# Attention heads in pairs: even and odd products issued in turn, wider blocks, shared banks

## The reference

```
moba:            p = softmax(mask(q k^T));                       o = p v
stick-breaking:  z = q k^T / 8;  log_beta = log_sigmoid(z)
                 later = reverse cumsum over keys of log_sigmoid(-z), the key itself left out
                 w = mask(exp(log_beta + later));                o = w v
forgetting:      z = q k^T / 8 + F[q] - F[k];  p = softmax(mask(z));  o = p v
out:             heads side by side @ w_o
```

## Time and profile before

| | us |
|---|---|
| median of 3 runs | 895.12 |
| lowest, highest | 892.17, 897.29 |
| profiled execution, own time | 894.86 |
| its span | 892.6 |
| PE busy in it | 862.9 |
| DVE busy in it | 646.9 |
| ACT busy in it | 491.5 |

### The profile page before, as it was taken

One profiled execution on the slowest core, in us unless ns is written; L12 is line 12 of the kernel. 1 busy time (PEld: TensorE's weight loads), 2 busy tenths in 40 slices (PEclk: granted clock), 3 DMA queues, 4 the chain that ended last, 5 costly groups with the idle time before them and its releaser, 6 DMA issues. The chain is left out here.

```text
span 892.6 us, 17122 instructions
## 1 busy us (share of the span) xinstructions
PE 862.9 (97%) x6968; PEld 823.1 (92%) x6968; DVE 646.9 (72%) x1332; ACT 491.5 (55%) x1015; POOL 21.2 (2%) x53
## 2 busy tenths in 40 slices
PE   6999998999999999999999997999999999999998
PEld 5788887999999999999999997878878999999998
DVE  5666666988998886999887868653634798666551
ACT  6744535777666666655545555543534676555441
POOL 1000000000000000000000007000000000000000
PEclk9999999999999999999999999977999999999999
DMA  9765365665665986699987875331304549755550
GB/s 303 245 189 184 103 190 188 215 204 197 212 208 170 314 290 211 202 316 356 308 304 258 279 232 142 116 119 48 117 25 143 189 143 329 237 189 178 189 177 24
DMA packets 151070, 179.46 MB, mean 201 GB/s; under 512 B 5712, under 2 KB 141136, under 8 KB 150992
## 3 DMA queue, kind: packets, MB, share of 16 engines
q1 hardware_dynamic: 149536, 177.65, 60.6%
q10 hardware_dynamic: 432, 0.68, 0.2%
q0 software_dynamic: 1024, 0.03, 0.1%
HBM read 177.27 MB, written 1.05 MB: 200 GB/s over the span
## 5 line engine op out<-in xcount | busy, mean ns | idle before, releaser
L894 DVE TENSOR_TENSOR wlo<-raw,whi 128x512 fp32r<-128x512 f32 x528 | 342.4, 683 | 60.5 <-ACT whi L659 59.7
L1257 PE MATMUL bank<-A,whi 128*128 128x256 f32 x1280 | 369.3, 289 | 14.1 <-DVE wlo L894 8.6
L659 ACT ACTIVATE whi<-raw 128x512 fp32r<-128x512 f32 x528 | 308.6, 621 | 110.8 <-PE bank L1259 101.9
L1258 PE MATMUL bank<-A,whi 128*128 128x256 f32 x1280 | 360.6, 282 | 0.0
L1259 PE MATMUL bank<-A,wlo 128*128 128x256 f32 x1280 | 360.4, 282 | 0.0
L1257 PEld LDWEIGHTS bank<-A,whi 128*128 128x128 f32 x1280 | 246.7, 193 | 18.5 <-issue 9.3
L1258 PEld LDWEIGHTS bank<-A,whi 128*128 128x128 f32 x1280 | 245.0, 191 | 1.0 <-issue 1.0
L1259 PEld LDWEIGHTS bank<-A,wlo 128*128 128x128 f32 x1280 | 244.8, 191 | 0.0
L1257 PE MATMUL bank<-Hhi,whi 128*128 128x256 f32 x528 | 147.0, 278 | 0.0
L1259 PE MATMUL bank<-Hhi,wlo 128*128 128x256 f32 x528 | 146.7, 278 | 0.0
L1258 PE MATMUL bank<-Hlo,whi 128*128 128x256 f32 x528 | 146.7, 278 | 0.0
(11 more groups left out here) (157 smaller groups left out, 920.8 us busy)
## 6 DMA issues: line engine op xcount, KB each, us to landing
mring<-in_w_mod SPq DMA_DIRECT2D x72, 512.0 KB, 6.0
raw<-in_ffn_w_up SPq DMA_DIRECT2D x22, 1024.0 KB, 5.1
raw<-in_w_gate SPq DMA_DIRECT2D x22, 1024.0 KB, 5.7
raw<-in_w_up SPq DMA_DIRECT2D x22, 1024.0 KB, 5.5
raw<-in_w_down SPq DMA_DIRECT2D x16, 1024.0 KB, 5.8
raw<-in_w_in SPq DMA_DIRECT2D x12, 1024.0 KB, 5.5
raw<-in_moba_w_qkv SPq DMA_DIRECT2D x11, 1024.0 KB, 6.3
raw<-in_ffn_w_down SPq DMA_DIRECT2D x8, 1024.0 KB, 7.2
```

The costliest lines, as they stand in the source:

```text
L659: act.activation(whi[:, i % SPL, k0:k1, 0:width], raw[:, i % RAW, k0:k1, 0:width], ACT.Copy).then_inc(s_whi, 1)
L894: dve.tensor_tensor(lo, raw[:, i % RAW, k0:k1, 0:width], hi.bitcast(F32), ALU.subtract).then_inc(s_wlo, 1)
L1257: pe.matmul(o, hi, xh, start=kg == 0, stop=False)
L1258: pe.matmul(o, hi, xl, start=False, stop=False)
```

## The change

Heads enter in pairs, every second call of `attend` at the earliest, and a pair's scores are issued ahead of the older pairs' steps. `scores` and `values` of both heads of a pair are issued product by product in turn, and a pair's transposes are spread over ages 2 and 3, `values` come at age 5. The scores' three blocks are laid in another order, so that one mask product of 256 columns (the same 128 twice) serves both diagonal blocks, and the stick-breaking scores and the `later` sums take one wide product in place of two or three narrow ones; values take two products a head in place of three. Scores have four banks (4, 5, 1, 3). For that the projections of the four phases around attention put both halves of a group into one bank, 0 or 2 (`halved`, `at`), apart from the first three groups of the phase `qkv3`. A padding is longer so that the buffers keep their places.

```diff
-LAST_AGE = 4
+LAST_AGE = 5
-S_BANKS = (4, 5)
+S_BANKS = (4, 5, 1, 3)
+HALVES = ("qkv1", "o1", "qkv3", "o3")
...
             if age == 0:
                 st.put("scores", n)
-            elif age == 1 and kind != "sb":
-                st.put("scale", n)
-            elif age == 2:
-                st.put("later" if kind == "sb" else "turn", n)
-                self.w_of[n] = len(self.w_of) + 1
+            elif age == 1:
+                st.put("stsum" if kind == "sb" else "scale", n)
+            elif age in (2, 3):
+                m = n + age - 2
+                st.put("later" if kind == "sb" else "turn", m)
+                self.w_of[m] = len(self.w_of) + 1
...
             old = list(flight)
-            if waiting and waiting[0][0] == "sb":
+            if waiting and (not flight or flight[-1][1] > 1):
                 enter()
-                for head in old:
-                    advance(*head)
-                st.put("stsum", flight[-1][0])
-                return
-            for head in old:
-                advance(*head)
-            if waiting:
-                enter()
+            for pair in old:
+                advance(*pair)
...
-        def pair_of(g):
-            return (0, 1) if g % 2 == 0 else (2, 3)
+        def halved(g):
+            return groups[g][0] in HALVES and g not in unnormed
+
+        def at(g, i, c0=0, c1=S):
+            if halved(g):
+                return banks[2 * (g % 2)][:, i * S + c0:i * S + c1]
+            return banks[2 * (g % 2) + i][:, c0:c1]
...
+            def first_passes(n):
+                first_pass(n)
+                first_pass(n + 1)
...
+            def peaks(n):
+                if heads[n][0] != "sb":
+                    peak(n)
+                    peak(n + 1)
...
+            def scales(n):
+                scale(n)
+                scale(n + 1)
...
+                for m in (n - 4, n - 3):
+                    if m in soft:
+                        need.wait_ge(s_exp, soft[m])
+                    elif m in stick:
+                        need.wait_ge(s_lb, stick[m])
...
+                if kind == "sb":
+                    for o0, o1, k0, q0 in ((P, 3 * P, 0, 0), (0, P, P, P)):
+                        for b, q, k in pair:
+                            pe.matmul(b[:, o0:o1], k[:, k0:k0 + P], q[:, q0:S], start=q0 == 0, stop=False)
+                    for b, q, k in pair:
+                        ins = pe.matmul(b[:, 0:S], identb[:, :], negs[:, :].unsqueeze(1).broadcast_to([P, 2, P]), start=False, stop=True)
+                        ins.then_inc(s_scores, 1)
+                    return
+                for o0, o1, q0 in ((0, S, P), (S, 3 * P, 0)):
+                    for b, q, k in pair:
+                        pe.matmul(b[:, o0:o1], q[:, q0:q0 + P], k[:, 0:o1 - o0], start=o0 == 0, stop=False)
+                if kind == "fox":
+                    i = (h - 8) // 2
+                    for o0, o1, q0 in ((0, S, P), (S, 3 * P, 0)):
+                        for e in range(2):
+                            r = slice(64 * e, 64 * e + 4)
+                            pe.matmul(pair[e][0][:, o0:o1], FA[r, i, q0:q0 + P], FB[r, i, 0:o1 - o0], start=False, stop=False)
+                for b, q, k in pair:
+                    ins = pe.matmul(b[:, P:3 * P], identb[:, :], negb[:, :].unsqueeze(1).broadcast_to([P, 2, P]), start=False, stop=True)
+                    ins.then_inc(s_scores, 1)
...
-                pe.matmul(b[:, 0:P], upn[:, :], spl[:, 0:P], start=True, stop=True)
-                pe.matmul(b[:, P:S], upn[:, :], spl[:, P:S], start=True, stop=False)
-                pe.matmul(b[:, P:S], negf[:, :], spl[:, S:S + P], start=False, stop=True)
-                pe.matmul(b[:, S:S + P], upn[:, :], spl[:, S:S + P], start=True, stop=True).then_inc(s_tpe, 1)
+                pe.matmul(b[:, 0:3 * P], upn[:, :], spl, start=True, stop=False)
+                pe.matmul(b[:, S:3 * P], negf[:, :], spl[:, 0:P], start=False, stop=True).then_inc(s_tpe, 1)
...
+                for t, o0, w0, w1 in ((0, 0, P, 3 * P), (1, P, 0, P)):
+                    for e in range(2):
+                        o, w = banks[O_BANK][64 * e:64 * e + 64, o0:S], W8[:, 2 * ((n + e) % 4) + 1, w0:w1]
+                        ins = pe.matmul(o, Vn[:, t, (h + e) * 64:(h + e) * 64 + 64], w, start=t == 0, stop=t == 1)
+                ins.then_inc(s_val, 1)
```

More of the change, by code:

```diff
@@ L227, in attend @@
         def attend():
-            for head in flight:
-                head[1] += 1
+            for pair in flight:
+                pair[1] += 1
             if flight and flight[0][1] == LAST_AGE:
@@ L599, in _ @@
             put(negb[:, :], 0.0)
-            keep(negb[:, P:2 * P], [[-1, P]], ALU.is_ge, NEG, 1)
+            keep(negb[:, :], [[-1, P]], ALU.is_ge, NEG, 1)
             put(blk[:, :], 0.0)
@@ L853, in values @@
             def values(n):
[L854 to L857, removed]
+                f = heads[n][2] // 2
+                need.wait_ge(s_val, n // 2 + 1)
+                act.activation(Ohi[:, f, :], banks[O_BANK][:, 0:S], ACT.Copy).then_inc(s_ohi, 1)
             def v_turned(ph, tile):
@@ L876, in _ @@
             part_of = {"hi": weights, "ain": a_in, "gq": norm_columns, "sq": squares, "norm": norm, "latey": late_hi, "modul": shift_hi,
-                       "ccol": condition, "evict": evict, "scores": first_pass, "turn": turned, "later": later,
+                       "ccol": condition, "evict": evict, "scores": first_passes, "turn": turned, "later": later,
                        "values": values, "vturn": v_turned, "qkn": qk_norm}
@@ L1042, in evict @@
                             ins = dve.scalar_tensor_tensor(
-                                out=y[:, part:S], in0=banks[bk[i]][:, 0:S - part], scalar=cvec[:, 2 - part, c:c + 1],
+                                out=y[:, part:S], in0=at(g, i, 0, S - part), scalar=cvec[:, 2 - part, c:c + 1],
                                 in1=y[:, part:S], op0=ALU.mult, op1=ALU.add)
@@ L1195, in values @@
             def values(n):
-                kind, ph, h = heads[n]
-                if h % 2:
-                    f = h // 2
-                    need.wait_ge(s_ohi, nth("values", n) // 2)
-                    dve.tensor_tensor(Olo[:, f, :], banks[O_BANK][:, 0:S], Ohi[:, f, :].bitcast(F32), ALU.subtract).then_inc(s_olo, 1)
+                f = heads[n][2] // 2
+                need.wait_ge(s_ohi, nth("values", n))
+                dve.tensor_tensor(Olo[:, f, :], banks[O_BANK][:, 0:S], Ohi[:, f, :].bitcast(F32), ALU.subtract).then_inc(s_olo, 1)
             def qk_norm(base):
@@ L1213, in _ @@
                        "hcol": gates, "gq": first_columns, "mod": mod_dot, "modout": mod_out, "xscale": scale_x, "evict": evict,
-                       "scores": peak, "scale": scale, "stsum": stick_sum, "later": later, "values": values, "qkn": qk_norm}
+                       "scores": peaks, "scale": scales, "stsum": stick_sums, "later": later, "values": values, "qkn": qk_norm}
             for step in st.list:
@@ L1255, in multiply @@
                     lo = wlo[:, i % SPL, kt, j * P:j * P + m]
-                    o = banks[pair_of(g)[j]][0:m, 0:ncol]
-                    pe.matmul(o, hi, xh, start=kg == 0, stop=False)
+                    o = at(g, j, 0, ncol)[0:m, :]
+                    pe.matmul(o, hi, xh, start=kg == 0 and not (j and halved(g)), stop=False)
                     pe.matmul(o, hi, xl, start=False, stop=False)
-                    ins = pe.matmul(o, lo, xh, start=False, stop=last and kt == nk - 1)
+                    ins = pe.matmul(o, lo, xh, start=False, stop=last and kt == nk - 1 and (j == 1 or not halved(g)))
                 if kt % 2 == 1:
@@ L1278, in scores @@
                 kind, ph, h = heads[n]
-                f, po = h // 2, 64 * (h % 2)
-                b = banks[S_BANKS[n % 2]]
-                q, k = QKV[po:po + 64, f, :], QKV[po:po + 64, 8 + f, :]
+                f = h // 2
                 emptied(need, max(qkv_group[ph, f], qkv_group[ph, 8 + f]))
                 need.wait_ge(s_const, n_const)
-                if n >= 2 and n - 2 in soft:
-                    need.wait_ge(s_exp, soft[n - 2])
-                elif n >= 2:
-                    need.wait_ge(s_lb, stick[n - 2])
-                if kind == "sb":
-                    for o0, k0, q0, cut in ((0, 0, 0, True), (P, 0, P, False), (S, P, P, True)):
-                        ins = pe.matmul(b[:, o0:o0 + P], k[:, k0:k0 + P], q[:, q0:q0 + P], start=True, stop=not cut)
-                        if cut:
-                            ins = pe.matmul(b[:, o0:o0 + P], identb[:, :], negs[:, :], start=False, stop=True)
-                    ins.then_inc(s_scores, 1)
-                    return
+                for m in (n - 4, n - 3):
[3 more added lines that the diff above has]
+                        need.wait_ge(s_lb, stick[m])
                 if kind == "fox":
```

103 lines of the change are left out of this document (46 added, 57 removed).

## The result

The changed kernel takes 864.42 us (median of 4 runs, 861.01 to 866.61) against 893.64 us (4 runs, 891.56 to 897.29) for the one before on the same chip: ratio 0.9665, 95% interval 0.9615 to 0.9716. The forecast was 869 us, with a range of 856 to 885. The profiled execution took 865.95 us with a span of 863.7, 28.9 less than before.

The account below looks back on a forecast made before the run. TensorE was taken as the bound, busy 862.9 of 892.6 us. From 894.86 us, 24.8 (fewer turns) plus 13.7 (overlap) less 12.2 (net waits), 26.3 in all, gave 869 us; range 856 to 885.

Parts of the forecast that it names:

- a gain from fewer turns: Attention scores and values: switches between 64-row and 128-row products are paid once per pair of heads, saving 24.8 us.
- the waits that the new order brings: Softmax quartets: TensorE waits for ScalarE's copy emptying the T bank; 14.0 us added, 12.2 net of waits that go.
- the second part: Scores and values of a pair: even and odd heads' products partly overlap on TensorE, saving 13.7 us.
- full overlap: Rival for scores and values: products side by side at full doubling, 862 us; chance 0.15, shared with a vanished slow stretch.
- scores, 12 pairs: Scores of eight moba and four stick-breaking pairs: 12.4 us saved with products one after another, overlap on top.
- forgetting, 4 pairs: Scores of four forgetting pairs: 2.36 us a pair against 4.00 without overlap, 6.5 us saved, overlap on top.
- values, 16 pairs: Value products of all 16 pairs: 0.37 us saved each without overlap, 5.9 us together, overlap on top.
- only the second pass of one can lie beside the first of the next: Scores and values: issue order limits overlap, so a pair's columns take 0.85 us instead of 1.28, saving 0.43 a step.
- The waits of `turn`: Second transposes in six softmax quartets: 1.25 us wait each for the T copy, about 1.2 more in the first quartet.
- Those of `vturn`: V transposes directly behind `turn` in six softmax quartets: 0.9 us wait each for the T copy.
- zero net: Clock: the slow stretch at 592.90 to 613.30, costing about 10 us, may vanish or move; no net change assumed.
- The slower rival: Waits of `turn` and `vturn` drop the clock to 1.2 GHz in softmax quartets, about 10 us each time; chance 0.05.

Follow-up runs that it names:

- e1: Changed kernel with all products of a pair's even head issued before all of the odd head's, in scores and values: 864.53 us.
- e7: Changed kernel with both heads' scores computed from the even head's q and k, so all on rows 0 to 63: 871.34 us.
- e9: e6 with a new pair entering at every third `attend` instead of every second: 846.59 us.
- e10: e9 with the conditioning row and its table loads on ScalarE one block of projections earlier: 844.27 us.
- e3: Changed kernel with two score banks and projections in whole banks, as before the change: 865.09 us.
- e4: Changed kernel with all widened products cut back to blocks of 128 columns: 863.59 us.
- e2: Changed kernel with the older pair's `turn` issued ahead of the new pair's scores in softmax quartets: 856.34 us.
- e6: Changed kernel with the edits of e2 and e5 together: 852.28 us.
- e12: e10 with scores unpaired: the even head complete with its mask, then the odd head; values stay paired: 864.29 us.
- e5: Changed kernel with `vturn` and the q/k norms issued one k tile (six projection products) later: 858.3 us.

## Why the prediction was right, and where its terms were off

It was right in its three parts: a gain from fewer turns, a gain from products side by side, less the waits that the new order brings. The size of the second part was the rival's, not its own: full overlap, for which it had 862 us. The sum was 26.3 us, the span fell by 28.9, and that this is so near is in part luck: the products brought 6.9 us more than forecast and the clock of the two profiled executions 3, against 5 lost in the projections, a term that the sum did not have, and 2 that stay unexplained. Term by term (gain in us):
```
                                 forecast            measured
scores, 12 pairs        12.4 + 5.2 = 17.6    12 x (2.84 - 1.19) = 19.8
forgetting, 4 pairs      6.5 + 1.7 =  8.2     4 x (4.00 - 1.57) =  9.7
values, 16 pairs         5.9 + 6.9 = 12.8    16 x (2.00 - 1.00) = 16.0
waits                              - 12.2    2.1 - 14.6         = -12.5
clock                                 0      13.4 - 10.4        =   3.0
projections' beat                     0                          - 5.0
sum                                  26.4                         31.0 (span: 28.9)
```
- **The overlap was mis-sized.** The step "only the second pass of one can lie beside the first of the next", 0.43 us a pair, failed: it took strict order of issue for a bound on what lies side by side. The whole of one head's columns lies beside the other's, 0.64 us in 0.86, and e1 shows that even grouped issue doesn't change it; e7 shows that the row groups do it. Over 32 steps that is 0.21 x 32 = 6.7 us. The Trainium skill, TensorE: Matmul & The Clock Gate, section "Part 3: Packing small matmuls", says that such products run concurrently; the trace agrees, with a second head at nothing, and this rival should have had the larger chance. What the value pairs alone are worth in time no run here isolates.
- **Turns and masks** came out as priced, once a pair: the forecast's 1.81 us for a pair one after another, less 0.64, is 1.17, measured 1.19; values 1.63 less 0.64 is 0.99, measured 1.00. Only the four FA/FB products were cheaper, 0.38 us with their turn against 0.55.
- **The waits of `turn`**, forecast 1.25 us, were 1.53 in the moba quartets, because in VectorE's list a rounding of 0.68 us stands ahead of the peak (116.20 above): exponentials begin 1.17 us behind the mask, not 0.76. In the forgetting quartets they were 1.17 and 1.25. In the first quartet 3.5, forecast 2.45. Those of `vturn`, forecast 0.9, were 0.67: PE was busy for 0.52 us from the start of the transposes, not 0.35. The errors nearly cancel (14.6 against 14.0). The forecast called itself wrong beyond 3 us of these waits a quartet: the mean is 2.4, but the first quartet has 4.2, where its own sum had 3.3. e9 and e10 confirm the cause: with the new pair's exponentials behind the copies, the waits go.
- **Four banks, wide blocks, halves: nothing** that can be told, as forecast (e3, e4). In e3 a wait of 2.5 us appears, and its projections on Hhi and Hlo are 4.5 us faster than after's (440.9), its mean clock lower (0.983), so that a few us could hide.
- **The clock** at zero net was a guess that lay near, for two movements that the forecast had as possible: the long stretch at 1.2 GHz behind the idle time at 590 shrank (3.4 us in place of 20.4), and three short ones came in the moba part behind the waits (granted 0.94 there, from 1.00). From the means, 0.015 x 892.6 = 13.4 us were lost before and 0.012 x 863.7 = 10.4 after. The 3.0 us belong to these two executions: the kernel before has a median of 0.988 over its other executions, and after has 0.988, 0.988 and 0.983 in its three others. Ten of the 25 have 0.990 or more, which leaves less than 18 us for all stretches at the lower level together, so that the long one isn't in every execution. The change brings nothing by the clock that can be told, as the forecast had it: here it had luck in that its rows are from an execution with such a stretch. The slower rival had the place right and the price too high: 3.4 to 6.8 us at half speed behind such a pair of waits, 1.7 to 3.4 us of time, not 10. e2, which has one longer wait per quartet in place of two, has a mean of 0.992.
- **A term that was not in it**: the projections on Hhi and Hlo, whose code is untouched, run slower. Rows by line, after and then before (count, busy us, mean ns):
```profile
L1276 PE MATMUL bank<-Hhi,whi 128*128 128x256 f32 x528 | 148.6, 281 | 0.0
```
```profile
L1257 PE MATMUL bank<-Hhi,whi 128*128 128x256 f32 x528 | 147.0, 278 | 0.0
```
Their code and place are the same. With the two other products of each step this is 445.4 against 440.4 us of modelled durations; from start to start the same products are 117.8 ns apart on average after and 114.8 before, 4.7 us over all 1584. The mean is 278 ns in four of the twelve experiments, 279 or 280 in the others, and goes with no edit: e6 has 278 and e9, differing in one number, 280. What sets it stays open.
- **Some 2 us** lie between the sum of the terms and the span. An estimate of what may be in them: in the profile an unhindered projection product starts 0.17 us ahead of the modelled end of the one before it (0.28 us long at a beat of 0.11), one that had to wait starts behind that end, and the idle time doesn't hold this difference. From 65.63, the last projection product ahead of a `turn` and `vturn` that wait, to 69.22, the second behind them, are 3.59 us; less two beats and the 2.20 us of idle time, 1.16. Alone, the two steps cost 0.34 (after, 97.29 to 97.85) and 0.45 (e12): 0.37 more, and up to 2.2 us in six quartets.

## What to carry to other kernels

Where two products use half of the array's rows (or of its columns) each, issue them next to one another and count the pair as one; the order within the pair doesn't matter, what must not stand between them is a product over all rows, such as a mask. Before a producer is moved ahead of older work, read the list of the engine behind it: here the copy that frees a buffer stood behind four exponentials; waits took back 12.5 of the 45.5 us won, and with four small changes of the order (e10) the gain in the span went from 29 to 50 us, most of it idle time. And a step's price read in a kernel that waits elsewhere is not its worth: the same edit cost 4 us in one surrounding and 17 to 20 in another. Before such a difference is put down to waits, the rows of untouched work have to be compared too: here they made up 5 us of it.

## What the runs showed of the hardware

- Eight f32 passes (four products of two passes each) take 0.86 us when four are on rows 0 to 63 and four on rows 64 to 127, four of them alone 0.85, and all eight on rows 0 to 63 1.50. The overlap is complete, also when the four passes of one row group are all issued ahead of the four of the other (0.87): the second pass of the even head's first product then starts 307 ns or more behind the first pass of the odd head, which stands behind it in the list. The Trainium skill, TensorE: Matmul & The Clock Gate, section "Part 3: Packing small matmuls", also says that matmuls start and end strictly in order of issue; by that the odd head's first pass would start behind the even head's last, after 0.645 us, and the mask at about 1.5 us as in e7. Between row groups the measurement contradicts the page.
- The same holds for products into output partitions 0 to 63 and 64 to 127 of one bank: x8 from 103.22 to the next product at 104.02, 0.80 us, for 2 x 384 columns of two passes.
- The granted clock was at the 1.2 GHz level from 69.7 to 73.1, although PE was busy in that stretch; what stood ahead were the waits of `turn` (1.53 us, to 67.44) and `vturn` (0.67 us, to 68.63). In e2 single waits of `vturn` of 1.7 us, to 67.45 and to 92.10, and in e5 single waits of `turn` of 1.5 us, to 66.32 and to 91.23, were followed by no such stretch. In e10, without any of these waits, the clock stayed at 1.00 throughout the moba heads (windows of PE):
```profile
22.00:132.00 110.00, 106.02 (x902) 1.00 0.68 224
132.40:139.20 6.80, 5.53 (x26) 0.50 0.00 0
```
  The stretch from 132.4 comes 19 us behind the last head's values; before and after have theirs at 156.0 and 151.6. So in these runs the falls within the moba heads go with the waits.
